# Both seams of the gate stage: routing tables turned between sixteen expert tiles, the first four value tiles and rows made between eight, gated activations in place

## What is computed

```
def peer(xn, w_query, sub_keys, u_tab, v_tab):
    ...
        s1 = jnp.einsum("thc,nc->thn", q[..., :half], k1)
        s2 = jnp.einsum("thc,nc->thn", q[..., half:], k2)
        v1, i1 = lax.top_k(s1, PEER_TOPK)
        v2, i2 = lax.top_k(s2, PEER_TOPK)
        ...
        top, pos = lax.top_k(cand, PEER_TOPK)
        eidx = jnp.take_along_axis(cidx, pos, axis=-1)
        g = jax.nn.softmax(top, axis=-1)
        hid = jnp.einsum("thkd,td->thk", u_tab[eidx].astype(jnp.float32), xt.astype(jnp.float32))
        a = g * jax.nn.gelu(hid, approximate=False)
        return jnp.einsum("thk,thkd->td", a, v_tab[eidx].astype(jnp.float32))
```

## Time and profile before

| what | us |
|---|---|
| median of three runs | 1867.72 |
| the profiled execution: its time | 1864.95 |
| its span, first to last instruction | 1863.4 |
| TensorE busy | 1691.0 (91%) |
| VectorE busy | 1397.9 (75%) |
| ScalarE busy | 776.9 (42%) |
| GpSimd busy | 570.6 (31%) |

### The profile page before, as it was taken

One profiled execution on the slowest core, in us unless ns is written; L12 is line 12 of the kernel. 1 busy time (PEld: TensorE's weight loads), 2 busy tenths in 40 slices (PEclk: granted clock), 3 DMA queues, 4 the chain that ended last, 5 costly groups with the idle time before them and its releaser, 6 DMA issues. The chain is left out here.

```text
span 1863.4 us, 30406 instructions
## 1 busy us (share of the span) xinstructions
PE 1691.0 (91%) x9914; PEld 1486.2 (80%) x9914; DVE 1397.9 (75%) x3179; ACT 776.9 (42%) x1195; POOL 570.6 (31%) x508
## 2 busy tenths in 40 slices
PE   5997898779799999779989999996899999999994
PEld 4997643449699999779989999996688888888883
DVE  3234267534389999968979888987898999999995
ACT  3222034221444433256657666663333333333333
POOL 0010280000354544433323333332433333333330
PEclk9998899899799999989999999998899999999997
DMA  3242361261343432379998998999999999999992
GB/s 112 97 174 94 121 214 46 83 232 43 116 143 111 138 115 82 124 259 350 345 376 304 366 354 332 380 338 361 363 386 387 384 384 384 384 384 389 385 385 81
DMA packets 195215, 470.82 MB, mean 253 GB/s; under 512 B 17922, under 2 KB 100482, under 8 KB 192558
## 3 DMA queue, kind: packets, MB, share of 16 engines
q1 hardware_dynamic: 124014, 240.30, 36.7%
q0 software_dynamic: 50944, 178.96, 26.0%
q10 hardware_dynamic: 20160, 50.34, 6.9%
HBM read 411.97 MB, written 61.32 MB: 254 GB/s over the span
## 5 line engine op out<-in xcount | busy, mean ns | idle before, releaser
L226 PE MATMUL hp<-mid_hi,uhi 128*128 128x384 f32 x1024 | 355.3, 347 | 12.0 <-issue 6.0
L227 PE MATMUL hp<-mid_lo,uhi 128*128 128x384 f32 x1024 | 345.7, 338 | 0.0
L228 PE MATMUL hp<-mid_hi,ulo 128*128 128x384 f32 x1024 | 344.4, 336 | 0.0
L226 PE MATMUL va<-vhi,ahi 128*128 128x512 f32 x768 | 299.6, 390 | 22.6 <-DVE alo L2010 22.6
L227 PE MATMUL va<-vlo,ahi 128*128 128x512 f32 x768 | 299.4, 390 | 0.0
L228 PE MATMUL va<-vhi,alo 128*128 128x512 f32 x768 | 299.2, 390 | 0.0
L2026 POOL DMA_INDIRECT gathered<-in_v_experts,idx_row x160 | 186.5, 1166 | 323.9 <-DVEq L1981 289.7
L1719 POOL DMA_INDIRECT gathered<-in_u_rows,idx_row x160 | 169.2, 1058 | 312.9 <-DVE hrow L1772 228.0
L226 PEld LDWEIGHTS hp<-mid_hi,uhi 128*128 128x128 f32 x1024 | 193.8, 189 | 17.3 <-DVE ulo L1785 8.6
L1316 ACT ACTIVATE uhi<-uw 128x1024 fp32r<-128x1024 f32 x128 | 135.7, 1060 | 151.9 <-PE hp L228 101.9
L1955 ACT ACTIVATE vhi<-vw 128x1024 fp32r<-128x1024 f32 x128 | 134.8, 1053 | 144.3 <-DMA vw<-in_v_experts 144.1
(11 more groups left out here) (328 smaller groups left out, 3306.2 us busy)
## 6 DMA issues: line engine op xcount, KB each, us to landing
uw<-in_u_experts SPq DMA_DIRECT2D x128, 512.0 KB, 6.7
vw<-in_v_experts SPq DMA_DIRECT2D x128, 512.0 KB, 10.6
hidden_values<-gelu_out ACTq DMA_DIRECT2D x128, 192.0 KB, 5.4
gate_matrix<-gst ACTq DMA_DIRECT2D x12, 2048.0 KB, 12.7
mid_hi<-hidden_values SPq DMA_DIRECT2D x32, 768.0 KB, 11.9
mid_lo<-gate_matrix SPq DMA_DIRECT2D x32, 768.0 KB, 16.6
pw<-in_w_qk SPq DMA_DIRECT2D x16, 512.0 KB, 3.5
qw<-in_w_query SPq DMA_DIRECT2D x16, 512.0 KB, 5.0
```

The source lines that it names most:

```text
L226: nc.tensor.matmul(out, a_hi, b_hi, start=first, stop=False)
L227: nc.tensor.matmul(out, a_hi, b_lo, start=False, stop=False)
L228: return nc.tensor.matmul(out, a_lo, b_hi, start=False, stop=last)
```

## The change

It moves work over the two borders of the gate stage, and changes where the value stage keeps its gated activations.

- **Counts.** `QX, GX = 16, 8`, so `GTI` is 12: 48 tiles in the query stage, 6 x 12 in the turns, 8 behind them. `MIX = 11` is the tail tile after which the tables are made.
- **First seam.** Exp of `GG` stands behind tail tile 11 on ScalarE, the three turnings behind tiles 12, 13 and 14 on TensorE (after `exin` and `table_prep`), their copies `slotT` beside them on ScalarE, the copies `x2p` behind tiles 0 and 1. SP issues the fetches of tail tiles 15 and later **behind** the spreads of the tables. VectorE's copies of the tables stand at the end of the query stage, and GpSimd issues the first five gathers of `u` there, three ahead of the split of one tile and two ahead of the next.
- **Second seam.** Behind the last turn, among the eight tiles: three of the last ten dot products for each tile, the rounding and rests of the first four `v` tiles, GELU of `hid`, the gates of the first four tiles (`weigh`), their `ahi` and `alo`, the first five gathers of `v`, four more `v` loads.
- **In place.** The gated activations overwrite the hidden values (`hd`; `af` is gone). The second gate buffer lies in the freed `uw`. A gate buffer is free only when the rests `alo` of its four tiles are made (the load waits for `alo` instead of `a`).

```diff
-        QX, GX = 8, 4
+        QX, GX = 16, 8
+        MIX = 11
...
+        def fetch_u_row(pool, r, slot, b):
+            if b == 0:
+                pool.wait_ge(gs["idx"], r + 1)
+            pool.wait_ge(gs["dot"], r * ROW + b + 1)
...
             @block.sync
...
-                for e in range(QX + UR):
+                for e in range(MIX + UR):
                     u_fetch(sp, RT * NH + e, e % UR)
                 sp.wait_ge(table_prep, 2)
...
+                for e in range(MIX + UR, QX + UR):
+                    u_fetch(sp, RT * NH + e, e % UR)
...
             @block.gpsimd
...
                 for e in range(QX):
                     u_split_lo(pool, RT * NH + e + 2, e % 2, (e + 2) % UR)
+                    if e == QX - 3:
+                        for b in range(3):
+                            fetch_u_row(pool, 0, 0, b)
+                    if e == QX - 2:
+                        for b in range(3, ROW):
+                            fetch_u_row(pool, 0, 0, b)
...
             @block.scalar
...
                     u_split_hi(act, RT * NH + e + 2, e % 2, (e + 2) % UR)
-                    if e == QX - 1:
+                    hidden_gelu(act, RT * NH + e, e % 2)
+                    if e < 2:
...
+                        nc.scalar.activation(x2p[:, e], x2r[:, e], ACT.Copy).then_inc(gs["x2p"], 1)
+                    if e == MIX:
                         act.wait_ge(s["exin"], 1)
                         nc.scalar.activation(GG[:], GG[:], ACT.Exp).then_inc(s["ex"], 1)
-                    hidden_gelu(act, RT * NH + e, e % 2)
+                    if MIX < e <= MIX + 3:
+                        act.wait_ge(gs["tr"], e - MIX)
+                        nc.scalar.activation(slotT[:, e - MIX - 1], tp, ACT.Copy).then_inc(gs["trev"], 1)
...
             @block.tensor
...
                     hidden_product(pe, RT * NH + e, e % 2)
+                    if MIX < e <= MIX + 3:
+                        i = e - MIX - 1
...
+                        pe.wait_ge(table_prep, (2, 2, 3)[i])
+                        if i:
+                            pe.wait_ge(gs["trev"], i)
+                        for t in range(TDT):
+                            last = nc.tensor.transpose(tp[:, t * P:(t + 1) * P], (I1, I2, GG)[i][:, t + 1], ident[:])
...
             @block.vector
...
+                last_dots = [(q, b) for q in range(2) for b in range(ROW)]
                 for e in range(GX - 2):
                     split_lo(NK - GX + e + 2, e % 2, (e + 2) % UR)
+                    for q, b in last_dots[3 * e:3 * e + 3]:
                         dve.wait_ge(gathered[b], 16 * (SR - 2 + q) + 16)
...
+                    if e == GX - 4:
+                        dve.wait_ge(s["dot"], SR * ROW + ROW)
+                        nc.vector.tensor_copy(idx_row[:, 0:BR], eidx[:, 0:BR]).then_inc(xs["idx"], BR)
+                        dve.sem_inc(xs["fetched"], ROW)
+                        dve.wait_ge(stored[1], 16 * (NI + 1))
+                        for c in range(GT):
+                            rest_of_v(dve, c, c)
                 dve.wait_ge(s["act"], 1)
                 nc.vector.tensor_tensor(coef[:], hid[:], sgate[:], ALU.mult)
+                dve.wait_ge(gld[0], 32)
+                for c in range(GT):
+                    weigh(dve, c, 0)
+                for c in range(GT):
+                    rest_of_a(dve, c, c, 0)
...
             @block.scalar
...
+                    if 1 <= e <= GT:
+                        act.wait_ge(stored[0], 16 * (NI + 1))
+                        act.wait_ge(vld[e - 1], 16)
+                        round_v(act, e - 1)
+                    if e == GX - 3:
+                        act.wait_ge(s["dot"], SR * ROW + ROW)
...
+                    if e == GX - 2:
+                        act.wait_ge(s["mm"], NI * N2 + RING)
+                        for c in range(GT):
+                            round_a(act, c, c, 0)
                 for i in range(2):
                     act.wait_ge(ge_stored[i], 8 * NK + 16)
...
             @block.sync
...
-                            sp.wait_ge(s["a"], (g - 1) * GT)
+                            sp.wait_ge(s["alo"], (g - 1) * GT)
                             load_gates(sp, g, q % 2)
```

More of the change, by code:

```diff
@@ L1300, in build @@
         nc.all_engine_barrier()
-        hp = [ps(query, f"hp{i}", [P, SEQ]) for i in range(2)]
+        hidden = ExitStack()
+        hp = [ps(hidden, f"hp{i}", [P, SEQ]) for i in range(2)]
         u_load = [sem(f"u_load{i}") for i in range(UR)]
@@ L2059, in _ @@
                 over_bodies(pe, body)
+        value.close()
+        query.close()
         with ExitStack() as st:
```

218 lines of the change are left out of this document (113 added, 105 removed).

## The result

The changed kernel took 1891.94 us (median of 4 runs, 1890.6 to 1894.69), the kernel before 1868.23 beside it (median of 4, 1864.65 to 1873.72). The ratio is 1.0132, with a 95% interval from 1.0116 to 1.0149. The profiled execution took 1890.6 us, its span 1889.0. The span before was 1863.4, so 25.6 us are to be found.

What follows compares the result with a forecast made beforehand. TensorE was taken as the bound, busy 1691.0 of 1863.4 us, with time to gain only where it stands. Seams and turns, 10.4 - 9.6 + 10.7, gave 11.5 us under 1867.72: 1856 us, range 1839 to 1869.

Steps and rivals of the forecast that it cites:

- First seam: From the query stage's tail to the gate stage: the gate stage starts at 829.6 us, a gain of 10.4 us.
- Second seam: From the last turn to the first value matmul: 45.4 us with eight tiles, a gain of 10.7 us.
- The turns: Six gate-stage turns of 12 tiles: 70.3 us each, between 68.7 and 74.7, a loss of 9.6 us.
- rival B: Turns: VectorE paces them; decides above 72.2 us a turn, at 73.0 the time is 1872 us; chance 0.16.
- VectorE's slowing: First seam: GpSimd's splits beside VectorE's eighth pass and final multiply add 6 and 1.5 us.
- SyncE's late tile 15: First seam: the fetch of tail tile 15 stands behind the spreads and lands at 813.8 us; TensorE waits for it.
- GpSimd's chain: End of the first seam: ScalarE's rounding, then GpSimd's splits and five gathers in a row, 15.1 us.
- The border: Between the query and gate stages: 0.7 us.
- rival D: Second seam does not shrink: store landing 12.8 us, gathers costing 8, seam 56, time 1867 us; chance 0.12.
- Value stage: From the first value matmul on: unchanged, 0 us, with the later gate load hidden; 550.1 us to the run's end.
- rival C: Value stage: gate buffers come late, 0.5 us a group, 15.5 less about 8 of lead, time 1864 us; chance 0.07.
- Rival A: Both seams in full: no slowing, turns of 68.7 us, time 1835 us; chance 0.20.

Runs made afterwards that it cites:

- e6: The changed kernel with each dot product of the turns cut to one element: 1874.29 us.
- e12: The changed kernel with each gate_matrix store of the turns cut to an eighth: 1929.4 us, including a copy that fills the matrix; turns of 69.2 us.
- e14: The changed kernel with GpSimd's splits of tail tiles 11 to 15 cut to one column: 1896.32 us (one run).
- e3: The changed kernel with product tiles 15 and 16 fetched on SyncE ahead of the spreading of the gates: 1889.08 us.
- e1: The kernel before with only the counts changed, 16 and 8 product tiles at the seams, and every other step at its old place: 1889.4 us, ratio 1.0094.
- e7: The kernel before with its old counts and tables, plus only the change's preparation of the value stage at the second seam: 1882.66 us, ratio 1.0062.
- e8: The changed kernel with value tiles, gates and value rows for the value stage held until the last hidden_values store has landed: 1893.12 us.
- e9: e7 with the loads for the value stage held until the last store has landed, and weighing ahead of the last five dots: 1876.95 us.
- e15: e9 with VectorE's last five dots ahead of the weighing: 1876.31 us.
- e17: The changed kernel with tiles 15 and 16 fetched before the gates' spreading, the first five row fetches in the gate stage, and gate_matrix stores in four parts: 1852.05 us.
- e10: The changed kernel with two more copies of 0.52 MB in each turn, read by nobody: 1897.74 us.

## Why the prediction was wrong

The span forecast was 1852.0. The trace puts the missing 37 us at: 6.1 ahead of the seams, 2.7 at the first seam, 17.4 in the turns, 10.6 at the second seam, 0.3 in the value stage.

**The turns: the step that failed.** The prediction put a turn at 70.3 us, "nearer the lower, because a busier VectorE waits less for others", a loss of 9.6 us. It was 27.0. The upper bound, 74.7, held the mean of 74.05; the choice inside it was wrong, and so was the reason. The rows read were TensorE's and VectorE's busy time. No term of the sum was for the 2.1 MB stores of a turn, and the earlier trace rows, with hidden_values stores landing after 5.9 us, was used for the second seam only. In turns of 14 tiles the stores' bursts were mostly covered: ScalarE waited 28.4 us for hidden_values stores, and yet TensorE lost only 7.3 to late one-hots. Two tiles less took that cover away: short rows are worth 2.6 us a turn with 14 tiles and 5.0 with 12, stores in parts about 1 and 5. The turn length at which rival B decides (over 72.2) was reached, but not by B's mechanism alone: without most of VectorE's work the turns were still 72.0 (e6), without the bursts they were 69.2 with all of it (e12). VectorE's load and the bursts work together: cutting the first gives back 12 us, cutting the second 29. Had the bursts been absent, the forecast of 70.3 would have been 1 us too high.

**First seam: right in its steps, wrong in what it was set against.** VectorE's slowing was put at 6 and 1.5 us and measured 6.3 and 1.9; e14 shows GpSimd's splits as its cause. SyncE's late tile 15 was there (e3: 3.1 us). GpSimd's chain, put at 15.1 us from ScalarE's rounding of tile 15 on, took 14.4 (820.6 to 835.0). The border was 3.1 in place of 0.7, and that is most of the miss: the gain was 7.7 for the 10.4 forecast. But e1 gained 13.7 with the tables left where they were. The forecast never priced that kernel, and so took for the gain of the turning what is the gain of eight more tiles.

The rule of the Trainium skill, page "SBUF — State Buffer" (Who interferes with whom), was weighed at 7.2 us for three meetings against the forecast's 6; the measured slowing is 6.3. The trace agrees with the rule in kind (8.4 us without the splits, 14.5 with them). It does not decide between the two counts.

**Second seam: rival D's number, in part by luck.** Put at 45.4, it took 56.0. Late rows ahead of the splits cost 7.65 us, put at 4; the last store and the border 9.7 from its issue, put at 6.6. Most of the rest is the clock, which the prediction gave no term: TensorE started again after 7.65 us of standing, and with the clock at 0.56 from 1300 to 1310 us (mostly 1.2 GHz) this product took 6.7 us in place of 4.2. D said 56 and named both waits, with 8 us for the rows and 12.8 for the store's landing. The store took less than that, and the clock, which D did not have, made up the sum. Nor did D say why no gain came. In e7, e8, e9 and e15 bytes fetched early delayed the seam's end, and bytes held delayed the value stage's start.

**Value stage:** nothing predicted, +0.3 measured; rival C did not come. **Rival A** needed turns of 68.7 and 1835 us; e17 has turns of 69.2 and yet takes 1852, as its second seam gives little.

**Still open.** Parts of a store may help in two ways at once: small stores behind them in ScalarE's queue can go earlier, and rows of GpSimd's queue meet a shorter burst. Both waits all but vanish together in e12 and e17, and nothing tried here separates them. e17 also has ScalarE's first two turns written out; that was not tried alone.

## What to carry to other kernels

Before shortening a loop, look at its largest transfer and at what was waiting behind it: work taken out of the loop also takes out the cover. Price the bare change of counts as a kernel of its own, or its gain is booked to the reordering that came with it. Where small stores and row fetches stand beside a store of megabytes, issue it in parts first; here that, with two edits at the first seam, made a change that lost 1.3% into one that gained 0.7%. In the kernel before, whose turns had more cover, it was worth 0.2%.

## What the runs showed of the hardware

*Some thousandths of a microsecond decided 4 us of the query stage.* From tile 0 to tail tile 0 it took 248.5 us in the kernel before and the four built on it, 251.6 to 251.7 in the changed kernel and eight built on it, and 255.4 to 255.6 in six others built on it, though no edit touches the instructions in it. VectorE's passes meet other GpSimd splits. After 80 us the same instructions took, in before and in after:

```profile
577.56 5.89 DVE L1589 TENSOR_TENSOR eq<-eq 128x1280 bf16<-128x1280 bf16 x3
```
```profile
580.23 8.14 DVE L1640 TENSOR_TENSOR eq<-eq 128x1280 bf16<-128x1280 bf16 x3
```

Here the engines' starts, counted from tile 0, differ by 0.2 to 0.3 us between the two. That the buffers' new places cause it is not shown. Between the changed kernel and e3 (255.6 us) the starts agree within 0.011 us, and still the paths part, 49 us behind tile 0. GpSimd's split and VectorE's run of three, in after and in e3:

```profile
548.63 2.59 POOL L1324 TENSOR_TENSOR ulo<-uw,uhi 128x1024 fp32r<-128x1024 f32 x1 [5.08 <-ACT uhi L1320]
547.02 1.94 DVE L1640 TENSOR_TENSOR eq<-eq 128x1280 bf16<-128x1280 bf16 x3
```
```profile
552.74 2.40 POOL L1324 TENSOR_TENSOR ulo<-uw,uhi 128x1024 fp32r<-128x1024 f32 x1 [5.08 <-ACT uhi L1320]
551.14 4.18 DVE L1642 TENSOR_TENSOR eq<-eq 128x1280 bf16<-128x1280 bf16 x3
```

In e3 the third VectorE instruction starts 0.008 us behind the split and takes 2.57 us; in after it starts 0.005 us behind and takes 0.33, and the split takes 0.2 us more. All twenty profiled executions sort by this one meeting: 2.57 to 2.58 us for VectorE in the six of over 255 us, 0.32 to 0.33 in the others. Each kernel has one profiled execution, so whether it falls the same way in every execution of a kernel is not known.

For a comparison this means that 3 to 7 us of a difference can come from a place that no edit touched, and stretches have to be compared and not only times: tile 0 itself began anywhere from 497.1 to 506.5 us in the profiled executions, on either side, e12 and its filling copy apart.

*A DMA share of 0.95 was no limit.* A turn of before ran at 355 GB/s with a share of 0.95, one of e10 at 373 with a share of 0.98, and one of e17, with the stores in parts, at 383 with a share of 1.00.
